# The value half of the token compression is spread over more pieces, up to the forgetting queries, and three chunks swap accumulators

## The reference, cut to what matters

```python
h = rms_norm(x, norm_mix) * (1.0 + sc_a) + sh_a
(cq, ckv, kr, fq, fk, fv, ff,
 nq, nkc, nvc, nks, nvs, nkw, nvw, ng) = jnp.split(h @ w_in, split_points, axis=-1)
o_mla = mla_mixer(cq, ckv, kr, ...)          # latent attention, 4 heads
o_fox = fox_mixer(fq, fk, fv, ff, fox_b_f)   # forgetting attention, 4 heads
o_nsa = nsa_mixer(nq, nkc, nvc, nks, nvs, nkw, nvw, ng, ...)   # sparse attention, 8 heads
...
def nsa_compress(tok, pos_emb, w1, w2):      # called for keys (nkc) and for values (nvc)
    ...                                      # 15 blocks of 32 tokens, each flattened to 4096
    return jax.nn.gelu(blk @ w1) @ w2        # w1: 4096 x 512
```

## Time and profile before

| | |
|---|---|
| time, median of 3 runs | 2399.65 us (2398.88 to 2400.06) |
| time of the profiled execution | 2400.43 us |
| its span | 2398.6 us |
| TensorE busy | 2312.1 us, 96% |
| VectorE busy | 1703.1 us, 71% |
| ScalarE busy | 1133.2 us, 47% |
| DMA, mean over the span | 266 GB/s |
| mean granted clock of TensorE | 0.987 |

### The profile page before, as it was taken

The page is one execution under the profiler, slowest core; times in us unless marked ns, Lnnn a source line. Parts: engine busy times, 40 slices in busy tenths (PEclk is TensorE's granted clock), DMA queues, the critical chain, the costliest instruction groups (busy, mean ns, idle before and its releaser), DMA issues.

```text
span 2398.6 us, 29297 instructions
## 1 busy us (share of the span) xinstructions
PE 2312.1 (96%) x11145; PEld 1904.2 (79%) x11145; DVE 1703.1 (71%) x2050; ACT 1133.2 (47%) x1576; POOL 19.2 (1%) x52
## 2 busy tenths in 40 slices
PE   3799999999999999999999999999999999999998
PEld 3687788878888888888878787887888888888887
DVE  7986788889877887887768667776675455455455
ACT  3253445455534434434446445465553443443453
POOL 1000000000000000000000000000000000000000
PEclk9699999999999999999999999999999999999999
DMA  9989977889988899989878897575787666666653
GB/s 366 384 270 365 356 262 229 295 278 370 332 299 296 295 319 318 319 316 301 302 233 279 286 343 250 158 253 179 249 270 220 184 188 189 192 186 193 188 188 124
DMA packets 321075, 637.08 MB, mean 266 GB/s; under 512 B 21068, under 2 KB 43048, under 8 KB 320552
## 3 DMA queue, kind: packets, MB, share of 16 engines
q1 hardware_dynamic: 314432, 625.49, 78.1%
q10 hardware_dynamic: 6504, 9.72, 1.2%
HBM read 633.00 MB, written 2.13 MB: 265 GB/s over the span
## 4 chain that ended last, share of the span: by engine, by line
PE 86%; DVE 7%; DMA 3%; issue 2%; ACT 1%; SPq 0%; POOL 0%; ACTq 0%; DVEq 0%; POOLq 0%
PE acc L1776 18%; PE acc L1778 18%; PE acc L1777 18%; PE pair L1776 7%; PE pair L1778 7%; PE pair L1777 7%; DVE ada_acc L1236 3%; PE bank_T L1638 2%; DVE w_lo L1306 1%; DMA arena<-in_ada_w 1%; PE acc L1800 1%; PE pair L1827 1%; PE bank_O L1638 1%; DMA cw_raw<-in_nsa_cmp_v_w 1%; PE pair L1835 1%
## 5 line engine op out<-in xcount | busy, mean ns | idle before, releaser
L1306 DVE TENSOR_TENSOR w_lo<-w_raw,w_hi 128x1024 fp32r<-128x1024 f32 (+3 forms) x764 | 905.8, 1190 | 385.9 <-ACT w_hi L799 384.9
L799 ACT ACTIVATE w_hi<-w_raw 128x1024 fp32r<-128x1024 f32 (+3 forms) x764 | 783.8, 1031 | 693.8 <-PE acc L1778 434.7
L1776 PE MATMUL acc<-w_hi,hT_hi 128*128 128x512 f32 (+3 forms) x1536 | 607.5, 396 | 15.7 <-DVE hT_lo L1421 8.2
L1778 PE MATMUL acc<-w_lo,hT_hi 128*128 128x512 f32 (+3 forms) x1536 | 589.1, 384 | 0.0
L1777 PE MATMUL acc<-w_hi,hT_lo 128*128 128x512 f32 (+3 forms) x1536 | 587.7, 383 | 0.0
L1236 DVE SCALAR_TENSOR_TENSOR ada_acc<-w_raw,silu_c,ada_acc 128x1024 f32<-128x1024 f32 x285 | 364.4, 1279 | 0.5 <-DVE small L1387 0.2
L1776 PEld LDWEIGHTS acc<-w_hi,hT_hi 128*128 128x128 f32 x1536 | 291.3, 190 | 85.2 <-issue 14.9
L1778 PEld LDWEIGHTS acc<-w_lo,hT_hi 128*128 128x128 f32 x1536 | 290.6, 189 | 56.0
L1777 PEld LDWEIGHTS acc<-w_hi,hT_lo 128*128 128x128 f32 x1536 | 291.9, 190 | 50.0 <-issue 0.5
L1776 PE MATMUL acc<-w_hi,uT_hi 128*128 128x512 f32 (+1 forms) x656 | 256.3, 391 | 0.0
L1778 PE MATMUL acc<-w_lo,uT_hi 128*128 128x512 f32 (+1 forms) x656 | 254.6, 388 | 0.0
(11 more groups left out here) (253 smaller groups left out, 1907.7 us busy)
## 6 DMA issues: line engine op xcount, KB each, us to landing
w_raw<-in_mlp_w SPq DMA_DIRECT2D x512, 512.0 KB, 4.7
w_raw<-in_ada_w SPq DMA_DIRECT2D x320, 512.0 KB, 5.7
w_raw<-in_w_in SPq DMA_DIRECT2D x112, 512.0 KB, 5.0
arena<-in_ada_w SPq DMA_DIRECT2D x64, 512.0 KB, 11.0
w_raw<-in_w_out SPq DMA_DIRECT2D x64, 512.0 KB, 5.5
cw_raw<-in_nsa_cmp_k_w SPq DMA_DIRECT2D x32, 512.0 KB, 6.7
cw_raw<-in_nsa_cmp_v_w SPq DMA_DIRECT2D x32, 512.0 KB, 7.0
w_raw<-in_w_in SPq DMA_DIRECT2D x16, 388.0 KB, 6.4
```

Source lines behind the costliest of these rows:

```text
L799: a.activation(w_hi[:, at % RING, :, 0:n], w_raw[:, i % RAW, :, 0:n], ACT.Copy).then_inc(hi_done, 1)
L1306: v.tensor_tensor(w_lo[:, at % RING, :, 0:n], w_raw[:, RING_NO["lo", Q] % RAW, :, 0:n], w_hi[:, at % RING, :, 0:n].bitcast(F32), ALU.subtr ...
L1776: pe.matmul(o, st_hi[:, kt + k, tok], wh, start=first and k == 0, stop=False)
L1778: mm = pe.matmul(o, st_hi[:, kt + k, tok], wl, start=False, stop=last and k == 1)
```

## The change

Before, the value half's clusters lie at positions 70-71, 74-75, 78-79, 82-83, 86-87, 89-90, 93-94 and 97-98, one or two pieces apart. After, they lie at 70-71, 75-76, 80-81, 84-85, 89-90, 94-95, 98-99 and 102-103, two or three pieces apart, and the last two are among the first pieces of `fq`. Since `acc1` is then still in use when `fq` begins, `fq` goes to `acc0`, `fk` to `acc1` and `fv` to `acc0`, and the first pieces of the output projection (`wo0`, `wo1`) change places accordingly. `fq` now begins at 100 on the accumulator that `nqb` has just used. The copies of `nqa` and `nqb` move up with their chunks, `hid1`, `vcmp` and `vrep` move back, and so does a block of modulation tiles in the second layer. Nothing is added or removed: each engine issues the same work.

```diff
@@ -30,7 +30,7 @@
     "vc": ("w_in", 3652, 512, 0), "uq0": ("uq", 0, 384, 1), "uq1": ("uq", 384, 384, 2),
     "vs": ("w_in", 4164, 512, 0), "cw1": ("cw1", 0, 512, 1), "kv0": ("ukv", 0, 512, 2), "kv1": ("ukv", 512, 512, 2),
     "vw": ("w_in", 4676, 280, 0), "nqa": ("w_in", 2368, 388, 0), "nqb": ("w_in", 2756, 512, 0),
-    "fq": ("w_in", 832, 512, 1), "fk": ("w_in", 1344, 512, 0), "fv": ("w_in", 1856, 512, 1),
+    "fq": ("w_in", 832, 512, 0), "fk": ("w_in", 1344, 512, 1), "fv": ("w_in", 1856, 512, 0),
     "wo0": ("w_out", 0, 512, 0), "wo1": ("w_out", 512, 512, 1), "wo2": ("w_out", 1024, 512, 2),
     "wo3": ("w_out", 1536, 512, 0),
 }
@@ -43,10 +43,11 @@
 ORDER += ["vc"] * 8 + ["uq0"] * 2 + ["uq1"] * 2
 
 ORDER += ["vs"] + ["vs", "cw1"] * 4 + ["kv0", "cw1"] + ["vs", "cw1"] * 3 + ["kv1", "cw1"]
-ORDER += ["vw", "cw1"] * 7 + ["vw", "cw1", "cw1"] + ["nqa", "cw1"] * 7 + ["nqa", "cw1", "cw1"]
-ORDER += ["nqb", "cw1"] * 5 + ["nqb"] * 3
-ORDER += ["fq"] * 8 + ["fk"] * 8 + ["fv"] * 8
-ORDER += ["wo0"] * 2 + ["wo1"] * 2 + ["wo0"] * 4 + ["wo1"] * 4 + ["wo2"] * 6 + ["wo0"] * 2 + ["wo1"] * 2
+ORDER += ["vw", "cw1"] * 7 + ["vw"] + ["cw1"] * 2
+for name, count in (("nqa", 3), ("nqa", 3), ("nqa", 2), ("nqb", 3), ("nqb", 3), ("nqb", 2), ("fq", 2)):
+    ORDER += [name] * count + ["cw1"] * 2
+ORDER += ["fq"] * 6 + ["fk"] * 8 + ["fv"] * 8
+ORDER += ["wo1"] * 2 + ["wo0"] * 2 + ["wo1"] * 4 + ["wo0"] * 4 + ["wo2"] * 6 + ["wo0"] * 2 + ["wo1"] * 2
 ORDER += ["wo2"] * 2 + ["wo3"] * 8
 
 
@@ -208,18 +209,18 @@
 
 
     for q, name in ((22, "cq"), (24, "ckv"), (28, "kc"), (34, "vc"), (36, "uq0"), (40, "uq1"), (48, "kv0"), (54, "vs"),
-                    (56, "kv1"), (72, "vw"), (89, "nqa"), (104, "nqb"), (112, "fq"), (120, "fk"), (128, "fv")):
+                    (56, "kv1"), (72, "vw"), (86, "nqa"), (100, "nqb"), (112, "fq"), (120, "fk"), (128, "fv")):
         side(F + q, ("evac", l, name), 4 if name in ("kc", "uq1") else 0)
     side(F + 75, ("hpre", l, 0), 4)
     side(F + 74, ("gates", l), 3)
     side(F + 76, ("gates2", l), 3)
     side(F + 91, ("forget", l), 3)
     side(F + 93, ("forget2", l), 3)
-    side(F + 101, ("hpre", l, 1), 1)
+    side(F + 104, ("hpre", l, 1), 1)
     steps = [(24, "cq0"), (25, "cq1"), (26, "ckv0"), (27, "kr"), (30, "nq7"), (31, "kcT"), (36, "vcT"), (37, "ks"),
              (38, "uq0n"), (39, "uq0r"), (42, "uq1n"), (43, "uq1r"), (50, "k0"), (56, "kw"), (58, "k1"), (76, "hid0"),
-             (81, "kcmp"), (91, "nqa0"), (92, "nqa1"), (96, "cum"), (102, "hid1"), (105, "nqb0"), (106, "nqb1"),
-             (107, "vcmp"), (108, "vrep"), (112, "csc"), (113, "fq0"), (114, "fq1"), (115, "cpt"), (118, "co0"),
+             (81, "kcmp"), (91, "nqa0"), (92, "nqa1"), (96, "cum"), (104, "hid1"), (105, "nqb0"), (106, "nqb1"),
+             (108, "vcmp"), (113, "vrep"), (112, "csc"), (113, "fq0"), (114, "fq1"), (115, "cpt"), (118, "co0"),
              (119, "co1"), (120, "co2"), (121, "co3"), (122, "omla0"), (123, "omla1"), (124, "fk0"), (125, "fk1"),
              (126, "onsa0"), (127, "onsa1"), (128, "onsa2"), (129, "onsa3"), (142, "ofox0"), (143, "ofox1")]
     for part in range(3):
@@ -246,7 +247,7 @@
         block_at(0, "M", 2, 132, 147, "adaM2")
     else:
         block_at(1, "G", 0, F + 4, F + 30, "rowG0")
-        block_at(1, "G", 1, F + 40, F + 109, "rowG1")
+        block_at(1, "G", 1, F + 40, F + 118, "rowG1")
         block_at(1, "H", 0, F + 118, F + 142, "rowH0")
     steps = [s for i, s in sorted(enumerate(steps), key=lambda e: (e[1][0], e[0]))]
     for q, name in steps:
@@ -260,9 +261,9 @@
     side(F + 126, ("decay", l), 4)
     side(F + 141, ("rms", l, "ofox"), 4)
     side(F + 40, ("cw2", l), 4)
-    for b, q in ((0, 66 if l == 0 else 20), (1, 106)):
+    for b, q in ((0, 66 if l == 0 else 20), (1, 107)):
         side(F + q, ("gate_bias", l, "G", b), 5)
-    for b, q in ((0, 89 if l == 0 else 34), (1, 117)):
+    for b, q in ((0, 89 if l == 0 else 34), (1, 120)):
         side(F + q, ("gate_out", l, "G", b), 5)
         side(F + 124 + b, ("gate_in", l, "G", b), 5)
     for b, q in ((0, 8 if l == 0 else -14), (1, 10)):
```

## The result

The changed kernel took 2416.52 us (median of 6 runs, 2411.74 to 2419.43) beside 2399.86 us (2398.66 to 2401.77) of the kernel before in the same session: ratio 1.0064, 95% interval 1.0053 to 1.0074. It is slower, and by more than twice what was forecast: 16.7 us for 7.4. The time lies outside the forecast's own range (2404 to 2410), in that of rival 1 (2410 to 2417), and 0.5 us inside the upper end of the range for 8 in 10. The profiled execution of the change took 2414.56 us, 14.1 more than that of before.

The account below looks back on a forecast made before the run. TensorE, busy for 96% of the span, bounds the kernel: 2400.43 - 8.1 us removed + 15.4 us added = 2407.7 us, forecast as 2407 us, 0.3% slower. Own range 2404 to 2410 us; 8 in 10, 2399 to 2417 us.

Parts of the forecast that it names:

- rival 1: Clock falls at the new waits, each costing up to 1.7 us; two to six give 2410 to 2417 us; chance 0.17.
- What is removed, waits: TensorE waits for loads, `nqa` copy, remainders and a gate row go; 8.1 us together with 1.7 of clock.
- rival 4: Loads not relieved: another cluster waits 2.8 us with slow clock, 4.5 us of gain missing, 2411.5 us; chance 0.05.
- What is added: Four waits in each layer, on ScalarE and VectorE chains that lost TensorE cover: 7.7 us a layer, 15.4 in both.
- (a): Piece 87 of `nqb` waits for its remainder: VectorE chain 6.3 us against 4.5 of TensorE work, wait 1.8 us.
- (b): Slot 10's scores wait for slot 9's exponentials: 4.5 us chain against 2.7 of TensorE work, wait 1.8 to 1.9 us.
- (c): Slot 12 waits for probability copy and exponentials behind cluster 102-103: 3.0 us chain, wait 2.3 to 2.4 in two pieces.
- (d): `fq0` waits for VectorE's copy of `vrep`, made after piece 116's remainder: wait 1.7 us.
- Rivals 2 and 3: 2: the two sides about cancel, 2400 us, chance 0.22. 3: chains mostly hidden, faster, 2395 us, chance 0.11.
- The clock: No clock fall counted behind new waits of 1.8 to 2.3 us, since the trace's 1.8 us wait had none.
- The sign that I had named for being wrong: Granted clock falling in several places where it had not before; also slot waits under 1 us or new DMA waits.

Follow-up runs that it names:

- The run with half the loads: Kernel before, with the value half loading only half of each piece's rows (values differ, engine work the same): 2395.35 us, ratio 0.9975.
- two different ways: Each against the changed kernel: latent attention's norm moved from 86 to 89, 2408.36 us; piece 87 issuing its remainder products last, 2409.00 us.
- the run with filled waits: Changed kernel with piece 87's remainder products last, plus TensorE repeating products in three other waits: 2410.16 us, ratio 1.0036.
- the new order: Pieces issue eight rounded-half products first, four remainder products last; the kernel before with this in every full piece took 2402.16 us, ratio 1.0006.
- the last run: Changed kernel with slots, norm, `vrep`, probability transposes and layer 0's gate rows moved, remainder products last only from piece 72: 2399.38 us, ratio 0.9996.

## Why the prediction was right in its sign and short in its size

**What is removed, waits.** Right in its sum. In the profile 2.76 us of the long cluster wait, 0.7 of layer 1's 0.9, 1.1 for the copy of `nqa`, some 1.2 of remainders and 0.4 of the row of gates are gone: 6.2 us for the 6.4 that I had without the clock. The run with half the loads shows that relief of this size reaches the end of the kernel. The cluster 70-71's wait, which I had at 0.7 us, was 2.46 us in one profile and 0.67 in the other; in the first the clock fell behind it (246 us), in the second ahead of it (239 us). No later cluster waits for a value load in either, and rival 4 falls.

**What is added.** Right in place, kind and size: (a) 1.88 and 1.8 us for 1.8; (b) 1.74 and 1.7 for 1.8 to 1.9; (c) 1.12 + 0.81 in each layer, 1.9 for 2.3 to 2.4; (d) 1.70 and 1.5 for 1.7. Together 14.3 us for 15.4. In (a) two omissions cancelled, which is luck: VectorE's chain took 6.65 us for my 6.3, since the row of gates (L1462, 0.34 us) that the order list shows there was not in the sum, and TensorE's own work took 4.9 us for my 4.5. Of the norm's 1.8 us, 0.8 is VectorE waiting for GpSimd (L765), so it is not VectorE's work alone. Rivals 2 and 3, which need hidden chains, fall.

**The clock.** This is the step that failed: "My sum has none behind the new waits of 1.8 to 2.3 us, being nearer to the second." One wait without a fall had been read as a rule. The sign that I had named for being wrong, falls in several places that had none before, came true at 246, 283 and 437 us. I also counted 1.7 us as gained from the fall at 286 us; in the changed kernel it stands at 283, behind wait (a). In the fourteen profiles, from 200 to 480 and from 1380 to 1600 us, TensorE waited 40 times for 1.7 to 2.7 us for another engine's work, and 16 of these waits have a slow stretch beginning at them or within 4 us; wait (a) of layer 0, with 1.9 to 2.1 us, has one in three profiles of four. Of 23 waits of 1.8 to 3.3 us for loads 14 have one. All 32 slow stretches of these windows begin at or within 4 us behind a wait of more than 1 us. By these counts a wait of the first kind costs some 0.7 us (0.4 of 1.7) more on the mean than it lasts; that is an estimate. It is rival 1, to which I gave 0.17, as a chance for each wait rather than a certainty. The Trainium skill's page "TensorE: Matmul & The Clock Gate", Part 1, says that only activity releases the throttle, which fits the 32 stretches behind waits, and that the number of slow matmuls at a kernel's start differs from run to run. The start was not compared here; in the middle of the kernel two profiles of one program have three and five slow stretches. Closing wait (a) in two different ways gave 8.2 and 7.5 us (5.8 within one session) where 3.6 and 2.2 us of waiting went, which supports it; that TensorE was at rest there, and not another thing at these places, is not shown by the run with filled waits.

**The balance of the profiled execution.** Waits 14.3 - 6.2 = 8.1 us; the clock 3.4 us (the stretch at 437 us, and the one at 246, which stood in a hidden place before); the start 0.3 us. These make 11.8 of 14.2 us. The other 2.4 us, about 1 us in each layer's stretch and 0.3 us behind it, I find in no wait of over 0.3 us: there are more places where transposes, a cluster and a slot meet, with 0.1 to 0.3 us each. That part is a remainder, not shown by an experiment. The median is 2 us above the profiled execution; its runs at a mean clock of 0.989 took 2411.7 to 2415.6 us, those at 0.987 2417.5 to 2419.4, so this may be one or two more slow stretches; the later four executions don't sort that way (2418.7 us at 0.989, 2412.8 at 0.988).

**The change as such.** With the four waits taken out again, it is even with the kernel before (2401.6 for 2402.2 us where both have the new order in every piece), though its loads wait less: in the last run's profile the 6.2 us stand against new waits ahead of transposes (2.7 and 1.4 us in layer 0) and of rows of gates (0.5 us in each layer), 0.7 us less ahead of one slot, and the 2.4 us of small rests. What makes the waits ahead of the transposes, the spreading of the gate rows or the later `vrep`, was not separated.

## What to carry to other kernels

On an engine that is busy for 96% of the span, the chains on the other engines must be summed for each place where work is taken out from between two dependent steps; done from rows of the trace, that sum held within 0.5 us at each of eight places here. In this kernel a wait of about 2 us on TensorE is better priced at its length and a share of the clock behind it; closing such waits gave back more than their length (8.2 us for 3.6, 5.8 for 2.2), part of it by chance. When the view names no releaser for a wait, as at slot 13, compare the ends of everything that the instruction needs. When loads are relieved by spreading their users, look first at which slots or copies stood on the old spacing.

## What the hardware did that I had not expected

Two executions of one program had three and five slow stretches with the same four added waits in them (spans 2412.8 and 2417.0 us). Six executions of another lay 10.7 us apart, with the mean granted clock between 0.986 and 0.991. In the start, the three profiles with the new order of products in every piece have the first cluster at 190.6 to 191.8 us, the eleven with the old order there at 188.3 to 190.9 us. TensorE waits 7.1 to 8.1 us for VectorE's sums of the modulation in the three, but 6.6 us also in one of the eleven that was not late (188.5 us), so what makes the start late stays open.
